# Attention scores two heads at a time, attention outputs by features, and spread parameter loads, in a two-block transformer kernel

## What is computed

```python
z = jnp.matmul(rms_norm(x, g_mix_pre), w_in)            # 256 x 3200
rq, rk, rv, rg, aq, ak, av, gu, gv = jnp.split(z, cuts, axis=-1)
y_ret = silu(rg) * merge_heads(retention(rope(rq), rope(rk), rv))        # 6 heads of 64
y_att = merge_heads(dilated_attention(rope(aq), rope(ak), av))           # 6 heads of 64
y_gm = spatial_gating(gelu(gu), gelu(gv), w_s, b_s)
x = x + rms_norm(jnp.concatenate([y_ret, y_att, y_gm]) @ w_out, g_mix_post)
...
def dilated_attention(q, k, v):    # three dilations; as one softmax: exp(scores + log(how many patterns hold the pair))
```

## Time and profile before

| | us |
|---|---|
| median of three runs | 1662.26 |
| lowest, highest | 1659.97, 1662.95 |
| the profiled execution | 1661.83 |
| its span in the trace | 1660.0 |

### The profile page before, as it was taken

How to read it: one execution, slowest core, us unless ns; L and a number is a source line. 1 busy time by engine, 2 the same in 40 slices (tenths; PEclk the granted TensorE clock), 3 DMA queues, 4 the chain that set the end, 5 groups by cost and what they waited for, 6 DMA issues and landing times.

```text
span 1660.0 us, 24380 instructions
## 1 busy us (share of the span) xinstructions
PE 1597.9 (96%) x9917; PEld 1215.8 (73%) x9917; DVE 776.1 (47%) x1285; ACT 606.0 (37%) x1089; POOL 476.1 (29%) x305
## 2 busy tenths in 40 slices
PE   6999999999999999999999999999999999999996
PEld 5888999869889998888787888898644444444442
DVE  5645333246463332379766666446533333332223
ACT  4544444444453443454536556333211111111111
POOL 4633445433234444400125665344300000000000
PEclk9999999999999999999999999999999999999998
DMA  7643987546439986443223333947999999999993
GB/s 263 201 153 106 276 248 222 190 129 218 138 102 265 265 256 228 136 106 102 76 77 101 103 103 103 304 127 250 370 413 422 423 422 423 423 422 424 421 422 154
DMA packets 244261, 397.87 MB, mean 240 GB/s; under 512 B 6725, under 2 KB 195585, under 8 KB 223280
## 3 DMA queue, kind: packets, MB, share of 16 engines
q1 hardware_dynamic: 237360, 365.45, 63.4%
q10 hardware_dynamic: 3760, 20.85, 3.2%
q0 software_dynamic: 3024, 9.95, 1.8%
HBM read 395.17 MB, written 1.05 MB: 239 GB/s over the span
## 4 chain that ended last, share of the span: by engine, by line
PE 80%; DMA 11%; DVE 4%; ACT 2%; issue 2%; POOL 1%; SPq 0%; ACTq 0%; DVEq 0%; POOLq 0%
PE ps L145 78%; DMA arena<-in_w_expert_up 4%; DMA ring<-in_w_expert_gate 4%; PE ps L147 2%; DMA ring<-in_w_out 1%; DVE split_r L151 1%; ACT split_r L149 1%; DVE arena L155 1%; ACT arena L149 1%; DMA ring<-in_w_branch_b 1%; DMA X<-in_x 1%; DVE arena L151 1%; POOL small L171 1%; POOL split_r L151 1%; DVE arena_r L151 0%
## 5 line engine op out<-in xcount | busy, mean ns | idle before, releaser
L145 PE MATMUL ps<-arena_r,split_r 128*128 128x256 f32 (+1 forms) x2984 | 459.7, 288 | 2.6 <-POOL split_r L151 2.6
L151 POOL TENSOR_TENSOR split_r<-ring,split_r 128x1024 fp32r<-128x1024 f32 (+1 forms) x142 | 334.8, 2360 | 305.4 <-ACT split_r L149 294.3
L145 PEld LDWEIGHTS ps<-arena_r,split_r 128*128 128x128 f32 x2984 | 393.3, 188 | 19.8 <-issue 14.6
L149 ACT ACTIVATE split_r<-ring 128x1024 fp32r<-128x1024 f32 (+1 forms) x293 | 296.5, 1019 | 293.7 <-PE ps L145 229.5
L151 DVE TENSOR_TENSOR split_r<-ring,split_r 128x1024 fp32r<-128x1024 f32 (+1 forms) x151 | 211.2, 1401 | 306.3 <-ACT split_r L149 294.3
L145 PE MATMUL ps<-split_r,arena_r 128*128 128x512 f32 (+1 forms) x1520 | 342.4, 378 | 3.6 <-POOL split_r L151 1.9
L145 PE MATMUL ps<-arena 128*64 128x512 f32 (+8 forms) x1472 | 310.3, 458 | 11.5 <-DMA arena<-in_w_expert_up 5.6
L145 PEld LDWEIGHTS ps<-split_r,arena_r 128*128 128x128 f32 x1520 | 274.6, 188 | 52.3 <-issue 8.4
L145 PEld LDWEIGHTS ps<-arena 128*64 128x64 f32 (+2 forms) x1472 | 137.2, 151 | 134.0 <-issue 119.2
L145 PE MATMUL ps<-hhh_r,split_r 128*128 128x256 f32 (+1 forms) x976 | 221.7, 316 | 0.0
L145 PE MATMUL ps<-ring,arena 128*64 128x512 f32 (+2 forms) x768 | 211.7, 576 | 7.1 <-DVE arena L151 2.3
(11 more groups left out here) (165 smaller groups left out, 1250.1 us busy)
## 6 DMA issues: line engine op xcount, KB each, us to landing
ring<-in_w_gate_up SPq DMA_DIRECT2D x88, 512.0 KB, 7.3
arena<-in_w_expert_up SPq DMA_DIRECT2D x15, 2048.0 KB, 29.4
arena<-in_w_expert_gate SPq DMA_DIRECT2D x15, 2048.0 KB, 29.1
ring<-in_w_expert_down SPq DMA_DIRECT2D x15, 2048.0 KB, 30.4
ring<-in_w_in SPq DMA_DIRECT2D x57, 512.0 KB, 5.3
ring<-in_w_expert_gate SPq DMA_DIRECT2D x13, 2048.0 KB, 27.1
arena<-in_w_ada SPq DMA_DIRECT2D x24, 1024.0 KB, 7.2
ring<-in_w_down SPq DMA_DIRECT2D x22, 1024.0 KB, 5.0
```

The costliest lines, as they stand in the source:

```text
L145: made = e.matmul(*a, **k)
L149: made = e.activation(*a, **k)
L151: made = e.tensor_tensor(*a, **k)
```

## The change

- PE: `two_scores` issues the scores of two heads (an even one and an odd one) together, small and large matmuls alternating: attention at s = 7, 11, 15, retention at s = 19, 20, 22.
- PE: `att_out(x)` makes the outputs of heads 2x and 2x + 1 by features: the values are the stationary operand (64 columns), the turned probabilities move (256 and 128 columns); head 2x goes to PSUM partitions 0 to 63 and head 2x + 1 to 64 to 127. It stands at s = 15, 19, 23. The outputs are then already in the layout that `out_quarter` takes, and the two `turn_y("att", ...)` are gone.
- ACT: `normalized(h)` multiplies the probabilities by the reciprocal sums before PE turns them: two activations of 128 and 256 columns per head, at k = 10 + 2h. `turned(h)` moves to k = 12 + 2h and `att_turn(h)` to s = 11 + 2h. Three copies of 256 columns (k = 17, 21, 25) replace two of 384.
- DVE: the mask's instruction scales by -0.125 and takes the minimum, and so gives the bias itself; the tensor_scalar is gone, and so is the multiplication in `attended`; the reciprocal moves to the start of step 10 + 2h (`inverse`). Three subtractions of 256 columns replace two of 384.
- POOL: `small_loads` is a generator; the two b_ada rows are still issued at k = 8, the other 15 DMAs one at a time in the gate loop of layer 0.

```diff
--- before.py
+++ after.py
-                def ret_scores(h):
-                    bk = take(("rsc", l, h), ("rsc", l, h, "kept"))
-                    K, Q = heads(0, h)
-                    t.matmul(bk[:, 0:256], K[:, 0:128], Q[:, 0:256], True, True)
-                    t.matmul(bk[:, 256:384], K[:, 128:256], Q[:, 128:256], True, True).then_inc(*sig(s_mm, ("rsc", l, h)))
+                def two_scores(name, a, h0):
+                    bks = [take((name, l, h), (name, l, h, "kept")) for h in (h0, h0 + 1)]
+                    KQ = [heads(a, h) for h in (h0, h0 + 1)]
+                    for second in range(2):
+                        for e, (K, Q) in enumerate(KQ):
+                            if name == "rsc":
+                                cuts = (slice(128, 256), slice(128, 256), slice(256, 384)) if second else (slice(0, 128), slice(0, 256), slice(0, 256))
+                                made = t.matmul(bks[e][:, cuts[2]], K[:, cuts[0]], Q[:, cuts[1]], True, True)
+                            else:
+                                cuts = (slice(128, 256), slice(0, 256), slice(128, 384)) if second else (slice(0, 128), slice(0, 128), slice(0, 128))
+                                made = t.matmul(bks[e][:, cuts[2]], Q[:, cuts[0]], K[:, cuts[1]], True, True)
+                            if second:
+                                made.then_inc(*sig(s_mm, (name, l, h0 + e)))
 
...
-                def att_scores(h):
-                    bk = take(("as", l, h), ("as", l, h, "kept"))
-                    K, Q = heads(1, h)
-                    t.matmul(bk[:, 0:128], Q[:, 0:128], K[:, 0:128], True, True)
-                    t.matmul(bk[:, 128:384], Q[:, 128:256], K[:, 0:256], True, True).then_inc(*sig(s_mm, ("as", l, h)))
-
                 def att_turn(h):
                     bk = take(("at", l, h), ("at", l, h, "kept"))
-                    t.wait_ge(*at("exp", l, h))
+                    t.wait_ge(*at("pn", l, h))
                     for k in range(3):
                         made = t.transpose(bk[:, tok(k)], PP[:, h % 2, tok(k)], ident)
                     made.then_inc(*sig(s_turn, ("at", l, h)))
 
-                def att_out(h):
-                    t.wait_ge(*at("at", l, h, "kept"))
+                def att_out(x):
+                    bk = take(("yt", l, "att", x), ("yth", l, "att", x), ("ytl", l, "att", x))
+                    for e in range(2):
+                        t.wait_ge(*at("at", l, 2 * x + e, "kept"))
                     for i in range(2):
                         t.wait_ge(*at("zst", l, 2, i))
-                    weighted("att", PT[:, h % 2, :], 2304, h)
+                    for i, q, k in ((0, slice(0, 256), slice(0, 256)), (1, slice(128, 256), slice(256, 384))):
+                        for e in range(2):
+                            c = 2304 + (2 * x + e) * 64
+                            made = t.matmul(bk[64 * e:64 * e + 64, q], Z[:, i, c:c + 64], PT[:, e, k], i == 0, i == 1)
+                    made.then_inc(*sig(s_mm, ("yt", l, "att", x)))
 
                 def turn_y(name, x, n, i):
                     bk = take(("yt", l, name, i), ("ytl", l, name, i))
-                    t.wait_ge(*at("ya", l, 5) if name == "att" else at("ym", l, name))
+                    t.wait_ge(*at("ym", l, name))
...
-                    if 7 <= s < 19 and s % 2:
-                        att_scores((s - 7) // 2)
-                    if 10 <= s < 22 and s % 2 == 0:
-                        att_turn((s - 10) // 2)
+                    if s in (7, 11, 15):
+                        two_scores("as", 1, (s - 7) // 2)
+                    if 11 <= s < 23 and s % 2:
+                        att_turn((s - 11) // 2)
                     if s == 11:
                         bk = take(("ws", l), ("wst", l))
                         t.wait_ge(*at("ws_in", l))
                         for g in range(4):
                             made = t.transpose(bk[:, tok(g)], WS[:, g, :], ident)
                         made.then_inc(*sig(s_turn, ("ws", l)))
-                    if 12 <= s < 24 and s % 2 == 0:
-                        att_out((s - 12) // 2)
+                    if s in (15, 19, 23):
+                        att_out((s - 15) // 4)
                     if s == 14:
                         turn_heads(3, 0, 0)
                     if s == 18:
                         turn_heads(4, 0, 1)
                     if s == 19:
-                        ret_scores(0)
-                        ret_scores(1)
+                        two_scores("rsc", 0, 0)
                     if 20 <= s < 26:
                         ret_out(s - 20)
-                        if s < 24:
-                            ret_scores(s - 18)
-                    if s in (25, 26):
-                        turn_y("att", 0, 3, s - 25)
+                        if s in (20, 22):
+                            two_scores("rsc", 0, s - 18)
 
...
-                    k = 0 if name == "gm" else i
+                    k = {"att": x, "gm": 0, "ret": i}[name]
...
                 def exps(h):
                     pp = PP[:, h % 2, :]
-                    s.wait_ge(*at("nm", l, h))
+                    s.wait_ge(*at("as", l, h, "kept"))
                     for i, (c0, n) in enumerate(((0, 128), (128, 256))):
-                        made = s.activation(pp[:, c0:c0 + n], pp[:, c0:c0 + n], ACT.Exp, bias=stat[:, 28 + 2 * h + i:29 + 2 * h + i], scale=0.125,
+                        made = s.activation(pp[:, c0:c0 + n], pp[:, c0:c0 + n], ACT.Exp, bias=stat[:, 28 + 2 * h + i:29 + 2 * h + i], scale=-1.0,
                                             accum_out=stat[:, 40 + 2 * h + i:41 + 2 * h + i])
                     made.then_inc(*sig(s_act, ("exp", l, h)))
+                def normalized(h):
+                    s.wait_ge(*at("is", l, h))
+                    for i, (c0, n) in enumerate(((0, 128), (128, 256))):
+                        pp = PP[:, h % 2, c0:c0 + n]
+                        made = s.activation(pp, pp, ACT.Copy, scale=stat[:, 52 + 2 * h + i:53 + 2 * h + i])
+                    made.then_inc(*sig(s_act, ("pn", l, h)))
 
                 def turned(h):
                     s.wait_ge(*at("at", l, h))
                     if h >= 2:
-                        s.wait_ge(*at("att", l, h - 2))
+                        s.wait_ge(*at("yt", l, "att", h // 2 - 1))
...
-                    if 11 <= k < 23 and k % 2:
-                        turned((k - 11) // 2)
+                    if 10 <= k < 22 and k % 2 == 0:
+                        normalized((k - 10) // 2)
+                    if 12 <= k < 24 and k % 2 == 0:
+                        turned((k - 12) // 2)
+                    if k in (17, 21, 25):
+                        x = (k - 17) // 4
+                        s.wait_ge(*at("yt", l, "att", x))
+                        s.activation(yt_part(x, 1, 0)[:, 0, :], B("yt", l, "att", x)[:, 0:256], ACT.Copy).then_inc(*sig(s_act, ("yth", l, "att", x)))
...
-                    if k in (26, 27):
-                        y_high("att", 0, 3, k - 26)
...
-                        made = v.ttr(PP[:, h % 2, c0:c0 + n], B("as", l, h)[:, c0:c0 + n], amask[:, c0:c0 + n], 1.0, -3e38, ALU.add, ALU.max,
-                                     stat[:, 16 + 2 * h + i:17 + 2 * h + i])
+                        made = v.ttr(PP[:, h % 2, c0:c0 + n], B("as", l, h)[:, c0:c0 + n], amask[:, c0:c0 + n], -0.125, 3e38, ALU.add, ALU.min,
+                                     stat[:, 28 + 2 * h + i:29 + 2 * h + i])
                     then(made, ("as", l, h, "kept"))
-                    v.wait_ge(*v.latest)
-                    then(v.tensor_scalar(stat[:, 28 + 2 * h:30 + 2 * h], stat[:, 16 + 2 * h:18 + 2 * h], -0.125, None, ALU.mult), ("nm", l, h))
-
-                def attended(h):
-                    c = 384 + h * 64
+                def inverse(h):
                     v.wait_ge(*at("exp", l, h))
-                    then(v.reciprocal(stat[:, 52 + 2 * h:54 + 2 * h], stat[:, 40 + 2 * h:42 + 2 * h]))
-                    v.wait_ge(*at("att", l, h))
-                    v.wait_ge(*v.latest)
-                    then(v.tensor_tensor(YY[:, :, c:c + 64], fold(B("att", l, h)[:, 0:128], 2), bc(stat[:, 52 + 2 * h:54 + 2 * h], 64), ALU.mult),
-                         ("ya", l, h), ("att", l, h, "kept"))
+                    then(v.reciprocal(stat[:, 52 + 2 * h:54 + 2 * h], stat[:, 40 + 2 * h:42 + 2 * h]), ("is", l, h))
...
-                        y_low("att", 0, 3, 0)
                         group_square("gmlp")
+                    if 10 <= k < 22 and k % 2 == 0:
+                        inverse((k - 10) // 2)
                     lo_to(n0 + k + 4)
+                    if k in (18, 22, 26):
+                        x = (k - 18) // 4
+                        v.wait_ge(*at("yth", l, "att", x))
+                        then(v.tensor_tensor(yt_part(x, 1, 1)[:, 0, :], B("yt", l, "att", x)[:, 0:256], yt_part(x, 1, 0)[:, 0, :], ALU.subtract), ("ytl", l, "att", x))
...
```

(11 more changed lines are left out.)

8 lines of the change are left out of this document (added).

## The result

The changed kernel took **1654.77 us** (median of 8 runs, 1652.5 to 1659.63) against 1662.59 us (8 runs) of the kernel before: a ratio of 0.995, 95% interval 0.9937 to 0.9963. The gain is 7.8 and 10.7 us; 13.8 were forecast, and 1654.77 lies 0.8 us above the range. The profiled execution is the fastest of the eight: 1652.5 us, span 1650.7, 9.3 less than the span before.

The account below looks back on a forecast made before the run. PE was taken to set the pace. 6.55 us a layer, 13.1 for two, plus 0.7 for parameter loads made 13.8 us off the profiled execution, 1648.0, or 1648.4 as the median; range 1645.5 to 1654.

Parts of the forecast that it names:

- Pairs of scores: PE's scores, two heads at 0.86 us: attention gains 2.5 us a layer, retention 1.7, plus 0.2 for fewer disturbed outputs.
- Attention outputs: PE's attention outputs: 0.80 us per two heads plus some 0.1 for the change of shape; gain 0.8 us a layer.
- second rival: Attention outputs on PE: the two column halves don't overlap, 1.5 us per pair, 4.2 us less gain, 1652.7; chance 5%.
- Transposes, interruptions, covered wait: PE's attention stretch, per layer: transposes gone 0.5 us, fewer interruptions 0.5, wait for DVE's key copies covered 0.35.
- Parameter loads: Layer 0: moving 15 of 17 POOL DMAs away gains 0.7 us; in the gate loop they cost nothing.
- Behind z: After z: the chain over gating, group norms and POOL's powers starts from PE's last retention output and shifts with it.
- third rival: Output pairs: late reciprocals or PSUM banks bring a new wait, 3 to 6 us in all, 1652 to 1654; chance 11%.
- What DVE saves: nothing by itself: DVE drops the tensor_scalar and the multiplication, six times each; DVE is not the bound, so no gain by itself.
- The DMA-bound end moves with the rest: End of the program: expert loads are issued after points PE reaches earlier by the same amount, so the end shifts too.
- The sum: Whole kernel: 6.55 us a layer, 13.1 for two, plus 0.7 for the parameter loads, 13.8 us in total.
- ACT's price: ACT's new normalization, at most 0.8 us a head: even steps about 2.2 us, odd 1.9; it fits PE's steps.
- fourth rival: ACT's normalization waits for DVE's reciprocal, the next high part comes late, PE runs dry; slower, 1667.8; chance 3%.

Follow-up runs that it names:

- e2: Changed kernel, PE doing the fourth head's retention output before attention's last output, DVE summing gating groups before its split of quarter 28; 1649.29 us, ratio 0.9912.
- e7: Changed kernel with retention's scores one head at a time again, attention's still in pairs; ratio 0.9934 to the kernel before.
- e3: Kernel before with only the paired scores of attention and retention; outputs, division and loads as before; ratio 0.9999.
- e4: Kernel before with only the small parameter loads spread out (`small_loads` as a generator); ratio 0.9997.
- e1: The changed kernel measured again, nothing altered; 1653.43 against 1664.09 us of the kernel before, ratio 0.9931.
- e8: The kernel before measured once more for a second trace, nothing altered; 1663.02 us, ratio 1.0.
- e11: e2 with ACT's third expert load issued one step later, behind its split of the last branch_b unit; 1647.9 us, ratio 0.9911.
- e17: Changed kernel with ACT's third expert load issued behind its split of the last branch_b unit; 1652.8 us, ratio 0.993.
- e12: e2 with one more unread DVE product of two SBUF operands per layer, behind the gating groups' mean squares; 77.63 us a layer.
- e5: Changed kernel with only PE's reordering: the fourth head's retention output ahead of attention's last output, behind quarter 23; ratio 0.9935.

## Why the prediction was wrong, point by point

- **Pairs of scores, right.** 0.86 us a pair; retention's pairs 2.03 us a layer (e2 against e7) where 1.9 was said, both kinds 4.4 us (e3, with its waits given back) where 4.2 + 0.2 was said.
- **Attention outputs, right.** 0.80 us a pair, and the change of shape put on with 0.1 us is there too, in the transposes in front of the pair: 0.42 to 0.48 us against 0.24 in front of a quarter and 0.32 in front of the old `att_out`. The second rival is out.
- **Transposes, interruptions, covered wait, right as a sum.** Four quarters in a row take 8.52 us (48.81 to 57.33 of layer 0), 2.13 each. With the wait for POOL taken away (e2) a layer went from 85.02 to 77.6, 7.4 us; the sum said 6.55. No run splits the 0.85 us that it was short.
- **Parameter loads, right.** 0.71 us (e4).
- **"Behind z": the step that failed.** It said that the chain over gating and POOL's powers "starts from PE's last retention output and shifts with it", and costed it at nothing. It starts earlier, at the Gelu behind ACT's copy of head 3, and the change removed 1.3 us of PE's work between its start and its end, put 0.8 us of PE's work in front of ACT's part, and moved POOL's power into a DVE split. The room was 1.29 us. Cost: 1.3 us a layer (e1 against e2), 2.6 in all; and in the profiled run 1.57 more for the low clock behind it, which comes and goes. With the step mended, e2 is 13.85 us ahead of before from first scores to the scan. That this meets the 13.8 is luck: its layers gave 8.1 and 7.4, and 1.7 went to the low clock ahead of layer 1. The wait is the third rival's mechanism, a new wait of 1 us, at a place that it did not name (it spoke of reciprocals and banks).
- **"What DVE saves: nothing by itself": not so for the pairs.** With the pairs alone (e3) PE waited 3.09 us for DVE, where the tensor_scalar took 4.25 us beside POOL's DMAs. The full change takes out both; no run parts them.
- **"The DMA-bound end moves with the rest": open within 2 us.** Of 10.63 us at the scan 8.35 were left at the router and 9.3 at the end; against the second trace of before (e8) the stretch from scan to router is only 0.3 to 0.5 us longer. The order of two issues on two queues, which the prediction didn't look at, flipped. This is between a loss of the change and chance: 11 of 11 times the meeting of the loads went with a late landing, but padding flips it both ways, and e11 and e17 show that removing it buys no more at the end than the measurement can tell.
- **The sum.** In e1, without low clock, the two layers are 6.78 + 6.10 = 12.9 us shorter than before (0.71 of it the loads), where 13.8 were said; less 2.0 in the branch stage that is 10.9, and the median was 10.7 less. The agreement is in part luck: e1's own trace started 0.75 us later, has 1.7 us more from the router to the end, and ends 8.4 us ahead of before's. In the first trace of after, 6.78 + 4.53 - 0.69 (a later start) - 2.28 = 8.3 at the router, and the first median was 7.8 less.
- **ACT's price, right.** ACT is busy 36.4 us where it was 32, and PE never waited for its normalization. The fourth rival did not come.

What stays open: what makes the expert load and the last branch_b load meet, and whether it costs anything at the end; and why the changed kernels without the gating wait have the low clock ahead of layer 1.

Lowest against the kernel before: e2 (1649.29 against 1664.09 us on one chip) and e11 (1647.9 against 1662.92 on another), both 0.991 of it. They can't be told apart. On e2's chip the changed kernel took 1653.43 (e1), but the intervals of the two ratios overlap.

## What to carry to other kernels

Work that is taken off the engine that sets the pace shortens also the time that a chain on the others had. So write down for each chain what stands on the pacing engine between its start and its end, before and after, and compare the removed time with the room. Here that alone (1.3 us against 1.29) left nothing to spare but would hardly have made a wait; the wait came because the chain also got longer. So ask of each step of the chain what will run beside it, for POOL above all which DVE instruction with two SBUF operands (e12). And where the room is used up, look first for an order that starts the chain sooner: two lines swapped took the wait away.

## What the runs showed of the hardware that was not expected

- A POOL instruction with operands in SBUF that came 0.17 us behind the start of a DVE instruction with two SBUF operands took 2.58 us instead of 1.68; beside a DVE sum over one operand 1.68. In e5 the power began 0.06 us ahead of a DVE split (107.13 and 107.19), and neither was longer (1.68 and 1.23).
- A DVE tensor_scalar on 128x2 numbers took 4.25 us (e3) while POOL issued four DMAs and split, and 1.25 us at the same place of layer 1.
- After the 1.02 us wait for POOL in layer 1 PE's clock fell to the lower level in one trace of the changed kernel and not in the other; after the 2.35 us wait ahead of layer 1 it was low in 12 of 20 traces, ten of them the changed kernels without the gating wait. It cost 1.5 to 1.7 us each time.
- Three transposes took 0.24 us between two weight quarters, 0.32 in front of the old `att_out`, 0.42 in front of the new one with its 64 stationary columns, and 0.48 where a pair of scores on 64 rows stood ahead of them as well.
- Where a load of 2 MB on ACT's queue was issued beside one of 512 KB on SP's, the small one landed in 9.8 to 11.8 us instead of 5 to 7.
- A float32 product of one moving column with a 128x128 stationary side took 0.43 us (48 in 20.64 us).
